# Strassen's seven products for the gate and up matmuls of feed-forward tiles 4 to 21

## The reference

```python
def swiglu(h, w_gu, w_down):
    gu = h @ w_gu                       # (512, 1024) @ (1024, 2 * 2816)
    g, u = gu[..., :D_FF], gu[..., D_FF:]
    return (jax.nn.silu(g) * u) @ w_down
# x = x + 0.5 * swiglu(rmsnorm(x, norm), w_gu, w_down)
```

## Time and profile before

| | us |
|---|---|
| median of 3 runs (2805.88 to 2809.49) | 2808.26 |
| profiled execution, its own time | 2806.19 |
| its span in the profile | 2804.3 |
| PE / DVE / ACT / POOL busy | 2777.9 / 1460.0 / 996.9 / 238.0 |
| granted PE clock, mean | 0.998 |

### The profile page before, as it was taken

One profiled execution on the slowest core, in us unless ns is written; L12 is line 12 of the kernel. 1 busy time (PEld: TensorE's weight loads), 2 busy tenths in 40 slices (PEclk: granted clock), 3 DMA queues, 4 the chain that ended last, 5 costly groups with the idle time before them and its releaser, 6 DMA issues.

```text
span 2804.3 us, 37976 instructions
## 1 busy us (share of the span) xinstructions
PE 2777.9 (99%) x15398; PEld 2214.6 (79%) x15398; DVE 1460.0 (52%) x2053; ACT 996.9 (36%) x1485; POOL 238.0 (8%) x188
## 2 busy tenths in 40 slices
PE   9999999999999999999999999999999999999999
PEld 7888876778888888888767888887878665788887
DVE  5333556564434543345756444466766876544435
ACT  4222444442223422234445322245344212332224
POOL 0000012010000100001301000001101431100001
PEclk9999999999999999999999999999999999999999
DMA  4222231122222223223112222221201221222222
GB/s 151 99 95 93 90 102 43 39 93 94 97 103 84 98 98 104 98 83 121 39 49 97 106 93 93 101 102 61 83 26 32 79 91 57 83 94 93 94 101 90
DMA packets 56973, 241.92 MB, mean 86 GB/s; under 512 B 6472, under 2 KB 10888, under 8 KB 38048
## 3 DMA queue, kind: packets, MB, share of 16 engines
q1 hardware_dynamic: 54896, 233.51, 24.2%
q10 hardware_dynamic: 1568, 6.64, 0.6%
q0 software_dynamic: 400, 0.23, 0.1%
HBM read 238.34 MB, written 2.10 MB: 86 GB/s over the span
## 4 chain that ended last, share of the span: by engine, by line
PE 92%; DVE 5%; ACT 1%; issue 1%; POOL 0%; DMA 0%; POOLq 0%; DVEq 0%; SPq 0%; ACTq 0%; PEldq 0%
PE psum L583 90%; DVE ring_lo L2120 1%; PE psum L1025 1%; DVE hid L2338 1%; ACT highs L1670 0%; POOL scr L2960 0%; DVE scr L2297 0%; DVE h_lo L2142 0%; DVE scr L2301 0%; ACT L1678 0%; DMA ring<-in_wgu 0%; PE psum L1260 0%; DVE scr L2422 0%; PE psum L1218 0%; DVE stat L2352 0%
## 5 line engine op out<-in xcount | busy, mean ns | idle before, releaser
L583 PE MATMUL psum<-highs 128*128 128x512 f32 (+2 forms) x3560 | 1282.2, 390 | 4.4 <-DVE ring_lo L2120 2.2
L583 PE MATMUL psum<-highs,ring_lo 128*128 128x512 f32 (+2 forms) x2712 | 1035.1, 389 | 0.0
L583 PE MATMUL psum<-h_lo,highs 128*128 128x512 f32 x2200 | 854.7, 388 | 0.0
L583 PEld LDWEIGHTS psum<-highs 128*128 128x128 f32 x3560 | 666.7, 188 | 154.3 <-issue 11.4
L2120 DVE TENSOR_TENSOR ring_lo<-ring,highs 128x2048 fp32r<-128x2048 f32 (+3 forms) x173 | 364.4, 2107 | 759.3 <-ACT highs L1670 688.6
L583 PEld LDWEIGHTS psum<-highs,ring_lo 128*128 128x128 f32 (+1 forms) x2712 | 508.5, 188 | 106.4 <-issue 0.2
L583 PEld LDWEIGHTS psum<-h_lo,highs 128*128 128x128 f32 x2200 | 412.5, 187 | 84.0 <-issue 0.5
L1670 ACT ACTIVATE highs<-ring 128x2048 fp32r<-128x2048 f32 x110 | 206.5, 1877 | 559.9 <-DMA ring<-in_wgu 537.7
L2960 POOL TENSOR_TENSOR scr<-scr 128x512 f32<-128x512 f32 x45 | 71.3, 1585 | 1719.5 <-ACT scr L1616 1716.4
L583 PE MATMUL psum<-highs,wdr_lo 128*128 128x512 f32 x488 | 190.0, 389 | 0.0
L2120 DVE TENSOR_TENSOR highs<-hid,highs 128x512 fp32r<-128x512 f32 x160 | 110.5, 693 | 143.2 <-ACT highs L1683 89.6
(11 more groups left out here) (425 smaller groups left out, 2918.5 us busy)
## 6 DMA issues: line engine op xcount, KB each, us to landing
ring<-in_wgu SPq DMA_DIRECT2D x105, 1024.0 KB, 5.5
wdr<-in_wd SPq DMA_DIRECT2D x110, 256.0 KB, 2.6
ring<-in_wd SPq DMA_DIRECT2D x25, 1024.0 KB, 4.8
ring<-in_wmix SPq DMA_DIRECT2D x28, 512.0 KB, 3.6
ring<-in_wmix SPq DMA_DIRECT2D x12, 1024.0 KB, 5.2
ring<-in_wproj SPq DMA_DIRECT2D x22, 512.0 KB, 3.5
ring<-in_wmix SPq DMA_DIRECT2D x8, 768.0 KB, 4.2
ring<-in_wgu SPq DMA_DIRECT2D x10, 512.0 KB, 5.6
```

The costliest lines, as they stand in the source:

```text
L583: return nc.tensor.matmul(o, w, r, start=start, stop=stop, skip_group_check=True)
```

## The change

In every feed-forward, tiles 0 to 3 stay as they were (`PLAIN = 4`). For tiles 4 to 21 the gate and up products are made together: the weights of a tile are seen as 2 x 2 blocks (lower or upper half of the width, gate or up), the activations as 2 x 2 blocks (lower or upper half of the width, tokens A = 0 to 255 or B = 256 to 511), and Strassen's form (Winograd's variant) takes seven block products of 4 width blocks x 3 matmuls x 256 columns, in place of eight. In the order of PE: A11 h11, S1 T1, S2 T2, A12 h21, S3 T3, then `down1(j-1)`, then S4 h22, A22 T4. The bank R collects A11 h11, S2 T2, S3 T3 and A22 T4; between them ACT copies its state three times (u1, u2, u3) for other sums, and PE's next product into R waits for that copy. Bank Q has S1 T1, is read by `up_second` (with u3), and then takes S4 h22 on top; bank G has A12 h21.

DVE makes the four sums of the raw weights S1 to S4 for each tile (512 elements each, S3 and S4 and A22 into 1536 adjoining elements of `ring`), and T1 to T4 once per feed-forward from x and the gain. ACT and DVE split 1024 elements of sums, 1024 of tops (A11, A12) and 1536 of rests (S3, A22, S4) in place of 2048 a tile. Gate and up are put together by DVE from banks and copies in halves of 256 tokens. `blocked_item` on SP waits for the splits of tile j-2 in place of `ring_free`. ACT's `high_rests(j)` waits for A22 of tile j-1 (`ring_free`), `high_sums(j+1)` for S1 and S2. Around it: buffers `ex` and `mixw` are shared, the pads are cleared by POOL before each use, the load of `wsmall2` into `mixw` is issued behind the last tile of the fourth feed-forward, and semaphores are merged.

```diff
@@ PE @@
+                def first_product(j, s, first=False):
...
+                        pe.wait_ge(ring_split, blocks_split(n0, j, 2))
+                        pe.wait_ge(gu_read, read_count(f, j, -4))
+                    block_product(R, a11, h11, True).then_inc(gu_done, 1)
+                def products(j, s, first=False, last=False):
...
+                        pe.wait_ge(gu_read, read_count(f, j, -3))
+                    block_product(Q, s1, r1, True).then_inc(gu_done, 1)
+                    pe.wait_ge(u_put, put_count(f, j, 1))
+                    block_product(R, s2, r2, False).then_inc(gu_done, 1)
+                        pe.wait_ge(gu_read, read_count(f, j, -1))
+                    block_product(G, a12, h21, True).then_inc(gu_done, 1)
+                    pe.wait_ge(u_put, put_count(f, j, 2))
+                    pe.wait_ge(ring_split, blocks_split(n0, j, 3))
+                    block_product(R, s3, r3, False).then_inc(gu_done, 1)
+                    down1(j - 1, 1 - s, f, o, False, False, (0, 1, 2) if last else (0, 1, 2, 3))
+                    pe.wait_ge(gu_read, read_count(f, j, 2))
+                    block_product(Q, s4, h22, False).then_inc(gu_done, 1)
+                    pe.wait_ge(u_put, put_count(f, j, 3))
+                    block_product(R, a22, r4, False).then_inc(ring_free, 1)
@@ ACT, one period @@
+                    silu(j - 1, 1 - s)
+                    high_rests(j, s)
+                    put_u(u1, r, j, 1, None if first else -3, 1)
+                    high_hid(j - 1, 1 - s)
+                    high_wd(j, s)
...
+                    put_u(u2, r, j, 3, None if first else -1, 2)
+                    if not last:
+                        high_sums(j + 1)
+                        high_tops(j + 1, 1 - s)
...
+                    put_u(u3, r, j, 5, None, 3)
@@ DVE, one period @@
+                    if first:
+                        up(PLAIN - 1, 1)
+                    else:
+                        up_first(j - 1, 1 - s)
+                    inner(j - 1, 1 - s)
+                    low_wd(j, s)
+                    low_rests(j, s)
+                    low_hid(j - 1, 1 - s)
+                    if first:
+                        low_t(t4_lo, blocks(t4), t4_hi, 4)
+                    if not last:
+                        sums_of_tops(j + 1, 1 - s)
+                        sum2(j + 1, 1 - s)
+                        sum4(j + 1, 1 - s)
+                    gate_first(j, s)
+                    if not last:
+                        low_sums(j + 1)
+                        low_tops(j + 1, 1 - s)
...
+                    up_second(j, s)
+                    gate_second(j, s)
@@ DVE, what it calls @@
+                    nc.vector.tensor_tensor(sums[:, 0, :], ring[:, sl, 1024:1536], ring[:, sl, 1536:2048], ALU.add).then_inc(s_made, 1)
+                    dve.wait_ge(s_made, sum_count(f, j, 1))
+                    nc.vector.tensor_tensor(ring[:, sl, 1024:1536], ring[:, sl, 0:512], ring[:, sl, 1024:1536], ALU.subtract)\
+                        .then_inc(s_made, 1)
...
+                    nc.vector.tensor_tensor(sums[:, 1, :], sums[:, 0, :], ring[:, (s + par) % 2, 0:512], ALU.subtract)\
+                        .then_inc(s_put, 1)
...
+                    dve.wait_ge(s_put, sum_count(f, j, 1))
+                    nc.vector.tensor_tensor(ring[:, sl, 2048:2560], ring[:, sl, 512:1024], sums[:, 1, :], ALU.subtract)\
+                        .then_inc(s_put, 1)
...
+                def up_second(j, s):
+                    dve.wait_ge(u_put, put_count(f, j, 3))
+                    nc.vector.tensor_tensor(up_r[:, B_TOK], psum[:, b + 1 + s, A_TOK], u3, ALU.add).then_inc(gu_read, 1)
+                    dve.wait_ge(gu_read, read_count(f, j, 2))
+                    nc.vector.tensor_tensor(up_r[:, B_TOK], up_r[:, B_TOK], rms_r[:, B_TOK], ALU.mult)
@@ SP @@
+            def blocked_item(f, n0, j, s):
+                sp.wait_ge(ring_split, blocks_split(n0, j, -3))
+                sp.dma_start(ring[:, s, 0:2 * KD * P], wgu[f, j]).then_inc(ring_in[s], 16)
@@ the first tiles @@
+                make_t1()
+                make_t2()
+                low_t(t1_lo, t1, t1_hi, 1)
```

More of the change, by code:

```diff
@@ L240, in build @@
         with ExitStack() as whole:
[L241 removed]
+            h, ring, wdr, d2, hid, scr, mixw, ex = (whole.enter_context(nc.sbuf_tensor(n, shape, F32)) for n, shape in (
                 ("h", [P, KD, S]),
@@ new lines, in swiglu @@
+                next_ring(0)
+                high_wd(0, 0)
+                copy_b11()
+                root(i, o + 3)
+                high_t(t1_hi, t1, 1)
+                put_r(i, o + 2)
+                silu(0, 0)
+                high_hid(0, 0)
+                next_ring(1)
+                high_wd(1, 1)
+                high_t(t2_hi, t2, 2)
+                high_t(t3_hi, t3, 3)
+                silu(1, 1)
+                high_hid(1, 1)
+                next_ring(2)
+                high_wd(2, 0)
@@ new lines, in swiglu @@
+                silu(2, 0)
+                high_hid(2, 0)
+                high_tops(PLAIN, 0, True)
+                high_wd(3, 1)
+                high_sums(PLAIN)
+                period(PLAIN, 0, first=True)
+                period(PLAIN + 1, 1)
+                with act.Fori(PLAIN // 2 + 1, NJ // 2 - 1) as jj:
+                    for s in range(2):
+                        period(2 * jj + s, s)
+                period(NJ - 2, 0)
+                period(NJ - 1, 1, last=True)
+                high_down(0)
@@ L2195, in swiglu, with low_hid, scaled_minus @@
-                with dve.Fori(1, NJ // 2 - 1) as jj:
-                    for s in range(2):
-                        body(2 * jj + s, s)
-                body(NJ - 2, 0, True)
-                body(NJ - 1, 1, True, DOWN_COLS[0])
+                def low_hid(j, s, ahead=1):
+                    dve.wait_ge(hid_high, 2 * f * NJ + j + ahead)
+                    low(hid_lo[:, s, :], hid[:, j, :], hid_hi[:, s, :].bitcast(F32), hid_split)
+                def scaled_minus(into, first, tokens, other):
+                    for k in range(4):
+                        last = nc.vector.scalar_tensor_tensor(out=blocks(into)[:, k, :], in0=x[:, first + k, tokens],
+                                                              scalar=gain[:, first + k:first + k + 1], in1=blocks(other)[:, k, :],
+                                                              op0=ALU.mult, op1=ALU.subtract)
+                    last.then_inc(t_made, 1)
@@ new lines, in swiglu @@
+                low_next_ring(0)
+                low_wd(0, 0)
+                rstd(i)
+                make_t1()
+                make_t2()
+                low_t(t1_lo, t1, t1_hi, 1)
+                dve.wait_ge(r_ready, stat_count(i))
+                gate(0, 0)
+                up(0, 0)
+                inner(0, 0)
+                low_hid(0, 0)
+                low_next_ring(1)
+                low_wd(1, 1)
+                make_t3()
+                gate(1, 1)
+                up(1, 1)
+                make_t4()
@@ new lines, in swiglu @@
+                inner(1, 1)
+                low_hid(1, 1)
+                low_next_ring(2)
+                low_wd(2, 0)
+                low_t(t2_lo, t2, t2_hi, 2)
+                gate(2, 0)
+                up(2, 0)
+                low_t(t3_lo, t3, t3_hi, 3)
+                inner(2, 0)
+                low_hid(2, 0)
+                low_wd(3, 1)
+                low_tops(PLAIN, 0, True)
+                sums_of_tops(PLAIN, 0, True)
+                sum2(PLAIN, 0, True)
+                sum4(PLAIN, 0)
@@ new lines, in swiglu @@
+                gate(3, 1)
+                low_sums(PLAIN, True)
+                period(PLAIN, 0, first=True)
+                period(PLAIN + 1, 1)
+                with dve.Fori(PLAIN // 2 + 1, NJ // 2 - 1) as jj:
+                    for s in range(2):
+                        period(2 * jj + s, s)
+                period(NJ - 2, 0)
+                period(NJ - 1, 1, last=True)
+                low_down(0)
+                up_first(NJ - 1, 1)
+                inner(NJ - 1, 1)
+                low_hid(NJ - 1, 1, 2)
```

374 lines of the change are left out of this document (278 added, 96 removed).

## The result

The changed kernel takes 3038.32 us (median of 4 runs, 3033.24 to 3040.49), the one before 2807.14 beside it; the ratio is 1.082, 95% interval 1.0801 to 1.0839. The forecast was 2943 us in a range of 2885 to 2985: the direction was right, the loss is 231 us where 135 were forecast. The span grew from 2804.3 to 3035.8 us, and the mean granted clock of PE fell from 0.998 to 0.964.

A forecast was written before the change was run, and what follows sets the result against it. PE's instruction stream was taken to bound the kernel. Steady tiles (16 x 1.46 us), tile 4 (+4.2) and tile 21 (-0.7) sum to 26.9, 134.5 for five feed-forwards; 2806.2 + 134.5 = 2940.7, median 2943 us, range 2885 to 2985.

The forecast's parts named there:

- PE's own price: PE in a new tile: 256-column matmuls at 0.120 us plus down matmuls, 12.80 us against 13.60, gaining 0.80 a tile.
- The queues: Steady tiles: DVE's and ACT's program order delays the read PE waits for; period 15.06 us, losing 1.46 against 13.60.
- The stall at `low_wd`: DVE waits at low_wd for ACT's high_wd, which stands behind two short copies and a long one; 2.1 us each period.
- rival 4: PE idle 2.2 us each period lowers its clock; a tenth of the time there adds 110 us, 3050 and up; 2%.
- A falling clock row: Sign of being wrong: in a 60 us feed-forward window the clock, forecast at 1.00, falls.
- The ends: First and last changed tiles of each feed-forward: tile 4 costs +4.2 us (end at 20.5), tile 21 gives -0.7.
- Rival 1: DVE's queue is not behind at low_wd or up_second; 72 us come back, about 2740 us; 7%.

The follow-up runs named there:

- e4: Changed kernel with DVE's low_wd behind low_rests, up_second ahead of low_sums and low_tops, and ACT's u3 ahead of high_sums and high_tops; 2752.4 us, ratio 0.9805.
- e1: Changed kernel with 16 useless 256-column matmuls ahead of PE's wait for up_second in tiles 5 to 20; 2957.3 us, ratio 1.0541.
- e5: Changed kernel with 16 useless matmuls ahead of PE's wait in tiles 5 to 20 and 24 in tile 4; 2954.3 us, ratio 1.052.
- e2: Changed kernel with DVE's low_wd moved behind low_rests, one line; 2844.3 us, ratio 1.0136.
- e8: Changed kernel with 8 useless matmuls ahead of PE's wait for up_second in tiles 5 to 20; 2961.0 us, ratio 1.0542.
- e9: Changed kernel with 4 useless matmuls ahead of PE's wait for up_second in tiles 5 to 20; 2958.8 us, ratio 1.0538.

## Why the prediction was wrong in size

- **PE's own price** (0.120 a matmul, 12.80 us a tile): right. e4's period is 12.79, with PE busy all the time.
- **The queues** (stall at `low_wd`, four sums, two low parts ahead of the read, period 15.06): right. The period is 15.12 without clock falls (e1, e5), and from `low_wd` to the read each DVE instruction stands within 0.1 us of its place. The stall at `low_wd` is 1.8 us where 2.1 were laid out. The edits that undo the order give 13.81, 13.45 and 12.79 where the same working gives 13.66, 13.6 and 12.80.
- **The clock**, rival 4: here the prediction failed. The step was "With 12.8 busy of 15 I give it 2%", by which the sum has no term for the clock and the range no room for it. Its reason was the windows of the earlier trace rows, which show PE pauses of some tenths at 1.00 and one stage at 0.86; neither holds a single pause of 2 us inside a busy stream, so the rows did not speak for the forecast. A falling clock row was named as a sign of being wrong, and it came. The trace of the kernel before does hold such a pause, which was not looked for (windows; the clock is the third number from the end):

```profile
1900.00:1939.78 39.78, 39.78 (x185) 30.74 (x183) 28.52 (x37) 27.51 (x40) 5.55 (x4) 1.00 0.22 67
1939.78:1942.01 2.23, 0.00 (x0) 0.00 (x1) 2.11 (x4) 0.00 (x0) 0.00 (x0) 1.00 0.55 147
...
1943.00:1944.00 1.00, 1.00 (x4) 0.46 (x3) 0.69 (x2) 0.68 (x1) 0.00 (x0) 0.63 0.00 0
1944.00:1946.00 2.00, 2.00 (x9) 1.48 (x8) 1.89 (x3) 0.37 (x1) 0.63 (x1) 0.50 0.00 0
```

  PE is busy for 39.78 us at full clock, pauses once for 2.23 us, and is at the lower level soon after, with no load landing. A pause of 2.2 us was forecast for every period, and this row shows what it can set off. In the changed kernel it did so in 57 of 80 periods, and in tile 4 in four of five; that costs 84 us by e5, in total 3038. The price on record was too high for the share of time: it put a tenth of the time at the lower level at 1.3 us a period (110 us, "3050 and up"), while the 57 stretches of about 3.4 us are 15% of the 80 periods and cost 0.97 us a period (16.09 against 15.12). The Trainium skill ("TensorE: Matmul & The Clock Gate", "What's actually happening") says that the lower clock is the default and activity lifts it. The rows agree (0.50 behind the pause, 1.00 again after some 3.4 us of work), but I read it as support, since the idle was short; the trace shows that 2.0 us can be enough.
- **The ends**: tile 4 was forecast at 20.5 us from the end of tile 3's up product to the end of its last product. In the first feed-forward, where no slow stretch follows, it is 84.57 - 64.11 = 20.46 us; the first row below starts right behind the up product of tile 3, and the one at 84.57 is the first matmul of tile 5:

```profile
64.11 0.28 PE L655 MATMUL psum<-highs 128*128 128x256 f32 x1
...
74.16 0.48 PE L655 MATMUL psum<-scr_r,highs 128*128 128x256 f32 x2 [1.40 <-issue]
...
81.60 0.39 PE L655 MATMUL psum<-highs 128*128 128x256 f32 x1 [3.03 <-DVE scr L2519]
...
84.57 0.28 PE L655 MATMUL psum<-highs 128*128 128x256 f32 x1
...
2970.03 0.70 PE L655 MATMUL psum<-highs 128*128 128x512 f32 x2 [0.78 <-DVE highs L2363]
```

  S4 h22 starts 17.49 us after the up product (forecast: 17.6), behind two pauses of 1.4 and 3.0 us. So tile 4 was right there. At the other end I had put up_first, inner and low_hid of tile 21 (2.9 us) under 3.4 us of PE work at no cost; PE waits 0.75 to 0.93 us there in each feed-forward (the last row is one of them), 4 us in all.
- **The account**: 231.5 us of span = 134.5 (forecast) + 84 (clock) + 5 (0.06 a period, 80 times) + 4 (the wait in front of tile 21's down product) + 4 not assigned.
- **Rival 1** (no queue is behind, about 2740) was not what happened, but its price was near: e4 is that case, 2752.

## What to carry to other kernels

When another engine must hand something back in the middle of PE's stream, lay out its queue instruction by instruction up to that hand-over and ask what stands ahead of it that nobody needs yet: the same instructions gave 3038 us in one order and 2752 in another. A pause of PE can cost more than itself: 1.5 us in every period cost nothing beyond the queue, 1.9 us cost some 80 us more. When you forecast a pause, look in the trace that you have for one of that length and read the clock behind it. Where there is none, give the clock a real chance and price it, and put it into the range.

## What the runs showed of the hardware

From 256 to 512 columns the distance of matmuls grows from 0.120 to 0.2267 us, 0.417 ns a column, which is one column a cycle at 2.4 GHz. So 256 columns are 107 ns, and 13 ns come on top. At the lower clock a 256-column matmul costs 0.212 us, a factor of 1.8, not 2: 256 columns at 1.2 GHz are 213 ns, and nothing is left on top.

The lower clock came behind single pauses of PE of 1.75 us and more, never behind the 240 of 0.38 to 1.55 us in tiles 5 to 20 of e2, e8 and e9. It could begin up to 1.7 us after PE had gone on, so that the slow matmuls need not be the first ones behind the pause. And 1280 matmuls without use made the kernel 81 us faster (e1).
